# Two-block transformer kernel: the second block's q and k are turned by VectorE and ScalarE instead of TensorE

## The reference, cut to what matters

```
h = einsum('bsd,de->bse', x, w_in_2)             # 2048 -> 8192 columns
qa, ka, va, ga, qb, kb, vb, gb = split(h)        # 8 pieces of 1024: 16 heads of 64 each, for two kinds of attention
ya = dilated_attention(qa, ka, va, t5_bias)      # s = q k^T * 0.125 + bias, softmax, times v
yb = neighbourhood_attention(qb, kb, vb, rpb)    # the same with another bias and mask
y  = concat(ya * silu(ga), yb * silu(gb))
x  = layer_norm(ALPHA * x + y @ w_out)
```

## Time and profile before

| | us |
|---|---|
| median of 3 runs | 2216.22 (2216.21 to 2216.39) |
| the profiled execution, its own time | 2216.83 |
| its span from the first to the last instruction | 2215.0 |

### The profile page before, as it was taken

The page is one execution under the profiler, slowest core; times in us unless marked ns, Lnnn a source line. Parts: engine busy times, 40 slices in busy tenths (PEclk is TensorE's granted clock), DMA queues, the critical chain, the costliest instruction groups (busy, mean ns, idle before and its releaser), DMA issues.

```text
span 2215.0 us, 24339 instructions
## 1 busy us (share of the span) xinstructions
PE 2203.9 (99%) x10186; PEld 1832.5 (83%) x10186; DVE 1382.4 (62%) x1301; ACT 990.9 (45%) x934; POOL 225.6 (10%) x253
## 2 busy tenths in 40 slices
PE   9999999999999999999999999999999999999998
PEld 8888888888888888888888888888888888888886
DVE  6577645545555545556855864864775677786755
ACT  7464654333333433344433433433444455555542
POOL 1023010000000000000100000000100122253201
PEclk9999999999999999999999999999999999999999
DMA  9555566677877776655655556566556755656663
GB/s 320 189 172 170 163 189 196 209 218 219 241 230 226 218 210 198 228 190 172 208 190 190 194 197 197 172 209 193 190 194 203 245 186 190 195 167 182 229 229 115
DMA packets 217100, 444.88 MB, mean 201 GB/s; under 512 B 9316, under 2 KB 10484, under 8 KB 216096
## 3 DMA queue, kind: packets, MB, share of 16 engines
q1 hardware_dynamic: 206976, 411.07, 57.0%
q0 software_dynamic: 9728, 32.18, 6.1%
q10 hardware_dynamic: 288, 0.10, 0.0%
HBM read 427.08 MB, written 12.06 MB: 198 GB/s over the span
## 4 chain that ended last, share of the span: by engine, by line
PE 99%; DVE 0%; POOL 0%; POOLq 0%; ACT 0%; issue 0%
PE acc L1421 32%; PE acc L1422 31%; PE acc L1423 31%; PE side L1431 1%; PE side L1509 1%; PE side L1445 1%; PE side L1495 1%; PE side L1481 1%; PE acc L1436 0%; PE side L1466 0%; PE side L1465 0%; PE side L1464 0%; PE side L1530 0%; PE side L1531 0%; POOL X L661 0%; PE side L1552 0%
## 5 line engine op out<-in xcount | busy, mean ns | idle before, releaser
L963 DVE TENSOR_TENSOR wlo<-raw,whi 128x2048 fp32r<-128x2048 f32 x380 | 893.5, 2352 | 638.2 <-ACT whi L678 637.6
L678 ACT ACTIVATE whi<-raw 128x2048 fp32r<-128x2048 f32 x380 | 727.6, 1915 | 748.6 <-PE acc L1423 731.1
L1421 PE MATMUL acc<-whi,setA_lo 128*128 128x512 f32 x1792 | 700.3, 391 | 0.0
L1423 PE MATMUL acc<-whi,setA_hi 128*128 128x512 f32 x1792 | 697.6, 389 | 0.0
L1422 PE MATMUL acc<-wlo,setA_hi 128*128 128x512 f32 x1792 | 697.6, 389 | 0.0
L1421 PE MATMUL acc<-whi,setB_lo 128*128 128x512 f32 x1280 | 501.9, 392 | 0.0
L1422 PE MATMUL acc<-wlo,setB_hi 128*128 128x512 f32 x1280 | 498.7, 390 | 0.0
L1423 PE MATMUL acc<-whi,setB_hi 128*128 128x512 f32 x1280 | 498.3, 389 | 0.0
L1423 PEld LDWEIGHTS acc<-whi,setA_hi 128*128 128x128 f32 x1792 | 336.6, 188 | 69.8
L1421 PEld LDWEIGHTS acc<-whi,setA_lo 128*128 128x128 f32 x1792 | 336.8, 188 | 69.2 <-DVE wlo L963 0.3
L1422 PEld LDWEIGHTS acc<-wlo,setA_hi 128*128 128x128 f32 x1792 | 336.7, 188 | 68.8
(11 more groups left out here) (208 smaller groups left out, 1019.4 us busy)
## 6 DMA issues: line engine op xcount, KB each, us to landing
raw<-in_w_in SPq DMA_DIRECT2D x188, 1024.0 KB, 5.3
raw<-in_w_ffn_up SPq DMA_DIRECT2D x64, 1024.0 KB, 5.3
raw<-in_w_ffn_down SPq DMA_DIRECT2D x64, 1024.0 KB, 5.1
raw<-in_w_gla_out SPq DMA_DIRECT2D x16, 1024.0 KB, 5.1
raw<-in_w_conv_out SPq DMA_DIRECT2D x16, 1024.0 KB, 5.1
raw<-in_w_o SPq DMA_DIRECT2D x16, 1024.0 KB, 5.1
raw<-in_w_out SPq DMA_DIRECT2D x16, 1024.0 KB, 5.2
t_scratch<-t5v POOLq DMA_DIRECT2D x8, 512.0 KB, 7.2
```

The costliest lines, as they stand in the source:

```text
L678: e.activation(whi[r][:, :, :], raw[r][:, :, :], ACT.Copy).then_inc(s_hi, 1)
L963: e.tensor_tensor(wlo[r][:, :, :], raw[r][:, :, :], asf(whi[r][:, :, :]), ALU.subtract).then_inc(s_lo, 1)
L1421: e.matmul(o, xl, whi[r][:, k, :], start=kk == 0, stop=False)
L1423: f = e.matmul(o, xh, whi[r][:, k, :], start=False, stop=kk == 15)
```

## The change

q2 and k2 no longer pass through TensorE. Four jobs over four steps take the place of `turn_qk2`:

- `block` (first step behind the unit): VectorE transposes all 32x32 blocks of `tmp` with one instruction on 128 lanes, 128x1024 elements, into `qTb` or `kTb`. A block transpose leaves each block in the 32 partitions that it came from. ScalarE then copies the 32 rows of quarter q = 0 to their four destination quarters of `qTr` or `kTr`, four instructions of 32x256 elements.
- `carry1`, `carry2`, `carry3`: the same four copies for q = 1, 2, 3. Behind those of `carry3` ScalarE waits for its own copies and rounds the whole 128x1024 to `qTa` or `kTa`; VectorE forms the low part.

`qTb`/`kTb` lie where `qTa`/`kTa` come to lie later, and `qTr`/`kTr` where `qTl`/`kTl` do. The side banks of PSUM that the transposes used fall to the next users in turn, and a `tmp` buffer is free once the block transpose has been made.

```
-         ..., "q2": ("none", "turn_qk2"), "k2": ("turn_qk2",), "y": ("none", "turn_y")}
+         ..., "q2": ("block", "carry1", "carry2", "carry3"),
+         "k2": ("block", "carry1", "carry2", "carry3"), "y": ("none", "turn_y")}
...
 # tmp_free
+            if kind in ("q2", "k2"):
+                return s_bt, block_of(TMPS[n]) + 1
...
 # ScalarE
-                    elif job == "turn_qk2":
...
-                        for b in range(2):
-                            hi_of(("turn", a, b), dst[:, :, :], b)
+                    elif job in ("block", "carry1", "carry2", "carry3"):
...
+                        q = int(job[-1]) if job != "block" else 0
+                        e.wait_ge(s_bt, block_of(a) + 1)
...
+                        for r in range(4):
+                            e.activation(to[32 * r:32 * r + 32, :, :, q, :], fr[32 * q:32 * q + 32, :, :, r, :],
+                                         ACT.Copy).then_inc(s_bm, 1)
+                        if q == 3:
+                            e.wait_ge(s_bm, 16 * block_of(a) + 16)
+                            e.activation(hi[g % 2][:, :, :], turned[g % 2][:, :, :], ACT.Copy).then_inc(s_bh, 1)
...
 # VectorE
-                    elif job == "turn_qk2":
...
+                    elif job == "block":
...
+                        e.wait_ge(*evacuated(a))
+                        if g >= 2:
+                            e.wait_ge(*full("scores", 8 * (g - 2) + 7))
+                        else:
+                            e.wait_ge(s_xf, 2)
+                        e.transpose(blk[:, :, :, :, :].rearrange("p k t r n -> p t k (r n)"),
+                                    tmp_of(a)[:, :, :].rearrange("p t (k n) -> p t k n", k=4)).then_inc(s_bt, 1)
+                    elif job == "carry3":
...
+                        e.wait_ge(s_bh, block_of(a) + 1)
+                        e.tensor_tensor(lo[g % 2][:, :, :], turned[g % 2][:, :, :], asf(hi[g % 2][:, :, :]),
+                                        ALU.subtract).then_inc(s_bl, 1)
...
 # TensorE, scores
-                    for name in ("q2", "k2"):
-                        for b in range(2):
-                            e.wait_ge(*seen("turn", UI[name, g], b))
+                    e.wait_ge(s_bl, 2 * g + 2)
```

More of the change, by code:

```diff
@@ L25 @@
 LATER = {"q": ("turn_qk",), "k": ("turn_qk",), "r": ("turn_r",), "cx": ("shift", "none", "conv0", "conv1"), "cb": ("turn_cb",),
-         "yb": ("turn_yb",), "wo": ("turn_wo",), "up": ("flip", "flip_split"), "q2": ("none", "turn_qk2"),
-         "k2": ("turn_qk2",), "y": ("none", "turn_y")}
+         "yb": ("turn_yb",), "wo": ("turn_wo",), "up": ("flip", "flip_split"), "q2": ("block", "carry1", "carry2", "carry3"),
+         "k2": ("block", "carry1", "carry2", "carry3"), "y": ("none", "turn_y")}
 LEVELS = (128, 64, 32, 16, 8, 4, 2, 1)
@@ L255, in two_block_program @@
         kTl = [at(f"kTl{i}", "A", 24 * KB + 4 * KB * i, [128, 4, 256], f32r) for i in range(2)]
+        qTr = [at(f"qTr{i}", "A", 8 * KB + 4 * KB * i, [128, 4, 256]) for i in range(2)]
+        kTr = [at(f"kTr{i}", "A", 24 * KB + 4 * KB * i, [128, 4, 256]) for i in range(2)]
+        qTb = [at(f"qTb{i}", "V", 4 * KB * i, [128, 4, 2, 4, 32]) for i in range(2)]
+        kTb = [at(f"kTb{i}", "V", 8 * KB + 4 * KB * i, [128, 4, 2, 4, 32]) for i in range(2)]
         qT = at("qT", "B", 0, [128, 8, 256])
@@ L350, in two_block_program @@
         s_fl, s_fh, s_fs = sem("s_fl"), sem("s_fh"), sem("s_fs")
+        s_bt, s_bm, s_bh, s_bl = sem("s_bt"), sem("s_bm"), sem("s_bh"), sem("s_bl")
         s_mb, s_nm, s_ex = sem("s_mb"), sem("s_nm"), sem("s_ex")
@@ L384, in tmp_of, with block_of @@
             return tmp[TN[u] % 3]
+        def block_of(u):
+            kind, g = UNITS[u]
+            return 2 * g + (kind == "k2")
         def tmp_free(u):
@@ L905, in scalar @@
                             root(i)
-                    elif job == "turn_qk2":
+                    elif job in ("block", "carry1", "carry2", "carry3"):
                         kind, g = UNITS[a]
[L908 to L912, removed]
-                        for b in range(2):
-                            hi_of(("turn", a, b), dst[:, :, :], b)
+                        blk, turned, hi = ((qTb, qTr, qTa) if kind == "q2" else (kTb, kTr, kTa))
+                        q = int(job[-1]) if job != "block" else 0
+                        e.wait_ge(s_bt, block_of(a) + 1)
+                        to = turned[g % 2][:, :, :].rearrange("p k (t q n) -> p t k q n", t=2, q=4)
+                        fr = blk[g % 2][:, :, :, :, :].rearrange("p k t r n -> p t k r n")
+                        for r in range(4):
[4 more added lines that the diff above has]
+                            e.activation(hi[g % 2][:, :, :], turned[g % 2][:, :, :], ACT.Copy).then_inc(s_bh, 1)
                     elif job == "att":
@@ L1364, in vector @@
                                                    in1=gfB[:, :], op0=ALU.mult, op1=ALU.mult).then_inc(s_xf, 1)
-                    elif job == "turn_qk2":
+                    elif job == "block":
                         kind, g = UNITS[a]
-                        hi, lo = ((qTa, qTl) if kind == "q2" else (kTa, kTl))
-                        for b in range(2):
-                            lo_of(("turn", a, b), lo[g % 2][:, :, :], hi[g % 2][:, :, :], b)
+                        blk = (qTb if kind == "q2" else kTb)[g % 2]
+                        e.wait_ge(*evacuated(a))
[6 more added lines that the diff above has]
+                    elif job == "carry3":
+                        kind, g = UNITS[a]
+                        hi, lo, turned = ((qTa, qTl, qTr) if kind == "q2" else (kTa, kTl, kTr))
+                        e.wait_ge(s_bh, block_of(a) + 1)
+                        e.tensor_tensor(lo[g % 2][:, :, :], turned[g % 2][:, :, :], asf(hi[g % 2][:, :, :]),
+                                        ALU.subtract).then_inc(s_bl, 1)
                     elif job == "att":
```

## The result

| | before | after |
|---|---|---|
| median, us | 2216.44 (6 runs, 2216.21 to 2216.98) | 2223.62 (6 runs, 2223.02 to 2225.74) |
| ratio | | 1.0033, interval 1.0021 to 1.0046 |
| the profiled execution, its own time | 2216.83 | 2223.24 |
| its span | 2215.0 | 2221.1 |

The changed kernel is 7.2 us slower. The time lies inside the range of 2210.5 to 2225.0, but 4.6 us above the forecast of 2219.0 and beyond the bound of 0.2%, so the likeliest class, no change, did not come.

The account below looks back on a forecast made before the run. TensorE was taken to bound the kernel (99% of the chain). Turns removed -7.04, waits +9.3, GpSimd +0.5 sum to +2.8 us: 2219.6 from the profiled 2216.83, less 0.6 for the median, 2219.0 us; range 2210.5 to 2225.0.

Parts of the forecast that it names:

- the likeliest class: Whole kernel: a difference within 0.2% (4.4 us), counted as no change, chance 0.44.
- 0.88 us a turn: TensorE: each removed turn of eight transposes saves 0.88 us, eight units 7.04 us.
- The rival at 2253.5: VectorE's block transpose not on all lanes at once: 7.0 us each, 11.5 us more a group; chance 0.04.
- the copies do not overlap: ScalarE's 32x256 copies, changing partition each time, run without overlap: 0.425 us each, 1.7 us a step.
- the YT rows: Two ScalarE YT copies in the old profile, starting in different partitions, 0.41 and 0.40 us apart at 0.38 length.
- the walk: Step-by-step timing of ScalarE, VectorE and TensorE over steps 320 to 327: 3.1 us of waits a group, 9.3 in all.
- wait at 325: TensorE waits 0.8 us for wlo of step 325, ready at 1838.15 against TensorE's arrival at 1837.3.
- wait at 326: TensorE waits 0.6 us more for wlo of step 326, done at 1844.2 against TensorE's arrival at 1843.6.
- wait at 327: TensorE waits 1.7 us more for wlo of step 327, behind k2's transpose and copies: 1851.35 against 1849.7.
- mask additions: GpSimd additions starting just ahead of a wlo on the path slow it by up to 1.3 us; 0.5 in all.
- The case with dear copies: ScalarE's copies cost 0.525 us each, adding 2.0 us a group: 2225.0 us, slower; chance 0.20.
- The case of overlapping copies: ScalarE's copies overlap, 0.31 us each, 1.25 a step, waits 1.7 us in all: 2210.9 us, faster; chance 0.20.

Follow-up runs that it names:

- Experiments 3 to 5: Changed kernel with only k2 by block turn, 2213.12 us; with only group 0, 2215.11; experiment 2 with both heads' bias DMAs issued before either mask addition, 2209.76.
- experiment 8: Changed kernel, but each copy writes the partition quarter it reads, so q and k are not fully turned; 2216.73 us, ratio 1.0000.
- experiment 1: Changed kernel with the first four copies of each k2 unit moved one step later, behind the block transpose's step; 2219.15 us, ratio 1.0013.
- Experiment 6: Changed kernel with GpSimd issuing both heads' bias DMAs before adding the mask to either; 2221.63 us, ratio 1.0023.
- experiment 2: Changed kernel with q2 and k2 copies spread over other steps, none in a transpose's step, k2's last two sets together; 2214.06 us, ratio 0.9988.

## Why the prediction was right or wrong

**Right: TensorE bounds, and 0.88 us a turn is what it gains.** Experiments 3 to 5 give it back to within 0.3 us wherever nothing is late (3.5 us for four, 1.5 for two, 6.8 for eight).

**Right: the block transpose on all lanes, 1.25 us.** It took 1.24. The rival at 2253.5 falls.

**Right, with a small error: the copies do not overlap.** The estimate was 0.425 us a copy and 1.7 a step; the trace shows 0.44 and 1.76 to 1.77. What decided for it, the YT rows, was the right evidence, and experiment 8 shows that it hangs on the partition that is written. The Trainium skill, "ScalarE: Activation LUTs", section "What ACT_TABLE_LOAD costs", has an overlap of 93 ns for ACTIVATEs in a row; the copies of experiment 8 agree (length 0.40, distance 0.31), those of the changed kernel, 0.415 long and 0.44 apart, do not.

**Right: where the waits are.** All nine stand at the steps named, and the idle time of ScalarE ahead of k2's copies is 3.51 us where 3.5 was worked out. That the one at 327 comes from ScalarE's copies, which wait for the transpose with the split behind them, is shown by experiment 1.

**Wrong: the size of the waits.** This is the step that failed: 0.8 + 0.6 + 1.7 = 3.1 us a group, 9.3 in all. The steps of the walk, moved by the 2.41 us by which this execution was early, beside the trace; a wait is counted from the start that TensorE could have made (0.23 us behind the one ahead) to the start that it made:

| | forecast | measured |
|---|---|---|
| TensorE ready for step 325 | 1834.92 | 1834.75 |
| end of `wlo` for step 325 | 1835.74 | 1836.20 |
| wait at 325 | 0.8 | 1.5 |
| wait at 326 | 0.6 | 0.4 |
| wait at 327 | 1.7 | 1.6 |
| restart behind the three waits | 0 | 0.5 |
| the group | 3.1 | 4.0 |

The 0.46 us at `wlo` of 325 are a sum of small terms. 0.15 are there before the first copy starts (1814.14 against 1816.4 - 2.41 = 1813.99). The three splits take 1.94 or 1.95 to whatever comes next where the walk gave 1.9, 0.13 together; the `wlo` of 324 takes 2.32 in place of 2.25; and all three sets of copies, with what they lose of the overlap ahead of them, add 0.1. Another 0.17 is a misreading: the walk took TensorE's arrival from the chain, which counts the last matmul to its drawn end, and not to where the next could start. The waits at 326 and 327 agree to 0.2. Then each wait costs TensorE about 0.15 us for its restart, in nine places, which the sum did not have at all. 4.0 against 3.1 in three groups is 2.7 of the 4.6 us.

**Wrong: GpSimd was costed as a neighbour, not as a supplier.** The prediction put in 0.5 us for mask additions that slow `wlo` down. In the changed kernel that cost nothing: all nine late `wlo` took 2.28 or 2.29 us. What the additions cost is that they come late. The chain of the changed kernel near the last scores passes through them:

```profile
2034.29 2.76 POOL bia L584
2037.05 1.77 POOL bia L581 x3
2038.82 5.13 DMA bia<-rb_scratch
...
2044.09 1.30 POOL bia L584
...
2045.47 0.70 DVE Sm L1412
```

A head's bias is an issue of four DMAs, their flight and an addition, one head after the other. The wait for it had stood in VectorE's waits before the change too (1.6 us at 2038.57, at no cost, since TensorE waited for nothing there). In the changed kernel it is

```profile
DVE Sm L1412 <- POOL bia L584: 4.6, 2, 3.2
```

and what stands behind `Sm` on VectorE reached TensorE: 0.8 us at 2053.9 and about 1.1 more in the third group, 1.9 together. Experiment 6 gets 2.0 us back, with the harm of its own edit in it. That is 1.5 more than the sum had. With the 2.7 above that makes 4.2 of the 4.6 us between forecast and median. The prediction had written that it would be wrong as a whole if TensorE waited for a side bank; this happened, for 1.0 us by the waits of TensorE.

**The chances.** The case with dear copies (2225.0) had the right size for the wrong reason: not dearer copies but restarts and biases made the waits long. That 2223.62 lies in the stated range is owed to the bound from that case. The case of overlapping copies was too low as well, by what experiment 8 can say: 2210.9 forecast, 2216.73 measured, though with the overlap only inside a set of four copies and not towards the split behind it. The prediction's own text says that 0.03 us a copy decides; the same holds for anything that adds 0.5 us to a group, and of such terms the walk had none. Three groups with a sum of small errors that all have one sign (nothing runs early that waits in turn) should have moved the middle up by some 2 us, and with it the likeliest class.

## What to carry to other kernels

Where TensorE bounds and a helper engine hands over its operand, work moved off TensorE is worth its full time only if the longest chain through the helpers in one step still ends ahead of it; place the new work so that no instruction waits at the head of a queue with the hand-over behind it (here the copies of k2: one step's shift gave 4.5 us). When the bounding engine becomes faster, look in the other engines' waits for those that cost nothing before, such as the bias here: they are next in line. In a walk through several engines add a term for each hand-over and for each restart, since they all have one sign.

## What the runs showed of the hardware

- In the rows here a ScalarE instruction overlaps its successor by about 0.1 us if both write from the same partition on, and not if the partition changes: 0.31 us apart with it, 0.44 without, for the same 32x256 copy.
- TensorE's first matmul behind a wait is 0.50 us long in place of 0.39, and the next starts 0.34 us behind it in place of 0.23 (1836.26 to 1836.60); with the intervals behind that a restart costs about 0.15 us.
- The granted clock fell to 0.50 for a little over 3 us at waits of 2.12 and 2.13 us (experiment 1) and 3.09 us (experiment 2), but not at 2.14 us in the changed kernel, nor at 2.41 and 2.03 in experiment 6. In experiment 1 it fell within 0.15 us of the wait's end, in experiment 2 0.6 us behind it. What decides between them was not settled. It may be part of why the changed kernel spreads over 2.7 us; the mean clocks on record, 0.998 for its slowest execution and 0.998 or 0.999 for the others, do not show it.
- The mask addition of GpSimd, 1.29 us alone, took 2.76 at 2034.29. The Trainium skill, "SBUF — State Buffer", section "SBUF: two separate sides", has VectorE and GpSimd take a shared pair of ports by an exclusive lock when VectorE has two inputs in SBUF and GpSimd reads SBUF, as here; the second then waits for the whole instruction of the first. The trace agrees for this row: a `wlo` of 2.29 us had started at 2033.61, and 1.29 us from its end are 2037.1, where the addition ended at 2037.05. The `wlo` of 2.87 us beside an addition and the two of 2.99 and 3.14 in experiment 6 are the same in the other direction, but each is 0.12 to 0.15 us shorter than a full wait would make it. No run here was made to test this.
